# Two decoder layers on one core: the S5 rotation goes back into PSUM with three drive banks, the S5 set-up is reordered, and the conditioning bias is spread over four column groups

## The reference

```python
mod = c_act @ w_ada[layer] + b_ada[layer]          # c_act = silu(c), 6*1024 columns a layer
sh_m, sc_m, gt_m, sh_f, sc_f, gt_f = split(mod, 6)
u = rms_norm(h, g_mix) * (1 + sc_m) + sh_m
```

```python
# S5, a group g of 16 channels with 64 states; dt = exp(log_dt)
mag = exp(lr * dt);  abar = mag * (cos(li*dt), sin(li*dt))
den = lr*lr + li*li;  nr = abar_r - 1
fr = (nr*lr + abar_i*li) / den;  fi = (abar_i*lr - nr*li) / den
bbar_r = fr*br - fi*bi;  bbar_i = fr*bi + fi*br
bu = ug @ bbar                                     # "drive"
x[t] = abar * x[t-1] + bu[t]                       # complex
y = xr @ c_re - xi @ c_im + d * ug                 # "read-out" and "skip"
y = gelu(y);  y = y * sigmoid(y @ w_glu + b_glu)
```

## Time and profile before

| | |
|---|---|
| median of three runs | 1721.92 us (1721.36 to 1724.17) |
| profiled execution | 1726.36 us |
| its span, first to last instruction | 1724.5 us |
| TensorE busy | 1609.7 us, 93% |
| VectorE busy | 1270.1 us, 74% |
| ScalarE busy | 1044.6 us, 61% |
| GpSimd busy | 79.2 us, 5% |
| mean granted clock of TensorE | 0.962 |

### The profile page before, as it was taken

How to read it: one execution, slowest core, us unless ns; L and a number is a source line. 1 busy time by engine, 2 the same in 40 slices (tenths; PEclk the granted TensorE clock), 3 DMA queues, 4 the chain that set the end, 5 groups by cost and what they waited for, 6 DMA issues and landing times.

```text
span 1724.5 us, 22990 instructions
## 1 busy us (share of the span) xinstructions
PE 1609.7 (93%) x7839; PEld 1269.1 (74%) x7840; DVE 1270.1 (74%) x1753; ACT 1044.6 (61%) x1401; POOL 79.2 (5%) x101
## 2 busy tenths in 40 slices
PE   4989979999898896899999999999999999999996
PEld 2535559999695554788888888888888888888885
DVE  6786245555445313889989989989989989989986
ACT  2203334444342542778878778778778778778775
POOL 7442000000000000000000000000000000000000
PEclk9889989999898897899999999999999999999998
DMA  9523745555653555699999999999999989999960
GB/s 324 205 98 123 286 165 177 183 177 184 227 189 106 189 194 205 227 359 340 349 347 356 353 349 348 352 332 372 354 332 363 357 334 365 353 336 369 347 246 26
DMA packets 208054, 469.66 MB, mean 272 GB/s; under 512 B 5316, under 2 KB 26102, under 8 KB 207878
## 3 DMA queue, kind: packets, MB, share of 16 engines
q1 hardware_dynamic: 206960, 466.80, 74.9%
q0 software_dynamic: 400, 1.09, 0.3%
q10 hardware_dynamic: 646, 1.16, 0.2%
HBM read 467.98 MB, written 1.05 MB: 272 GB/s over the span
## 4 chain that ended last, share of the span: by engine, by line
PE 84%; DVE 7%; ACT 3%; issue 2%; DMA 1%; SPq 1%; DVEq 0%; POOL 0%; ACTq 0%
PE ps L790 22%; PE ps L792 21%; PE ps L791 21%; PE ps L796 3%; PE ps L813 2%; PE ps L1283 2%; DVE w_lo L1798 2%; PE ps L857 2%; PE ps L1054 2%; ACT work L1694 1%; DMA ring<-in_w_ada 1%; PE ps L974 1%; PE ps L945 1%; PE ps L871 1%; PE ps L925 1%
## 5 line engine op out<-in xcount | busy, mean ns | idle before, releaser
L1798 DVE TENSOR_TENSOR w_lo<-ring,w_hi 128x1024 fp32r<-128x1024 f32 (+4 forms) x600 | 672.8, 1154 | 92.0 <-ACT w_hi L1488 79.1
L1488 ACT ACTIVATE w_hi<-ring 128x1024 fp32r<-128x1024 f32 (+4 forms) x600 | 601.2, 1008 | 216.8 <-PE ps L792 214.5
L790 PE MATMUL ps<-w_hi,e_hi 128*128 128x512 f32 x896 | 356.7, 398 | 9.7 <-DVE w_lo L1798 9.7
L792 PE MATMUL ps<-w_hi,e_lo 128*128 128x512 f32 x896 | 350.7, 391 | 0.0
L791 PE MATMUL ps<-w_lo,e_hi 128*128 128x512 f32 x896 | 349.8, 390 | 0.0
L1798 DVE TENSOR_TENSOR w_lo<-ring_more,w_hi 128x1024 fp32r<-128x1024 f32 x192 | 228.9, 1221 | 40.5 <-ACT w_hi L1488 38.1
L1488 ACT ACTIVATE w_hi<-ring_more 128x1024 fp32r<-128x1024 f32 x192 | 201.6, 1067 | 70.7 <-PE ps L792 70.7
L790 PEld LDWEIGHTS ps<-w_hi,e_hi 128*128 128x128 f32 x896 | 168.9, 188 | 46.1 <-DVE w_lo L1798 13.2
L792 PEld LDWEIGHTS ps<-w_hi,e_lo 128*128 128x128 f32 x896 | 168.6, 188 | 36.6
L791 PEld LDWEIGHTS ps<-w_lo,e_hi 128*128 128x128 f32 x896 | 169.1, 189 | 33.6
L790 PE MATMUL ps<-w_hi,eT_hi 128*128 128x512 f32 x448 | 176.7, 395 | 5.6 <-DVE w_lo L1798 5.6
(11 more groups left out here) (281 smaller groups left out, 1743.5 us busy)
## 6 DMA issues: line engine op xcount, KB each, us to landing
ring<-in_moe_w_gate SPq DMA_DIRECT2D x48, 2048.0 KB, 9.8
ring<-in_moe_w_up SPq DMA_DIRECT2D x40, 2048.0 KB, 10.1
ring<-in_moe_w_down SPq DMA_DIRECT2D x32, 2048.0 KB, 10.0
ring<-in_w_ada SPq DMA_DIRECT2D x24, 2048.0 KB, 8.7
ring_more<-in_moe_w_down SPq DMA_DIRECT2D x24, 2048.0 KB, 7.8
ring_more<-in_moe_w_up SPq DMA_DIRECT2D x16, 2048.0 KB, 9.9
ring_more<-in_moe_w_gate SPq DMA_DIRECT2D x8, 2048.0 KB, 9.4
ring<-in_ff_w_gate SPq DMA_DIRECT2D x8, 1408.0 KB, 6.3
```

Of the source, the lines that this page charges most:

```text
L790: mm(o, xh, wh, start=start, stop=False)
L792: return mm(o, xl, wh, start=False, stop=stop)
L1488: fn(w, src, ACT.Copy).then_inc(hi_ready, 1)
L1798: V.tensor_tensor(w_lo[0:n, c, 0:f], src, w_hi[0:n, c, 0:f].bitcast(F32), ALU.subtract).then_inc(lo_ready, 1)
```

## The change

**Turn.** The sine product goes to `rotB` in SBUF as before; then the cosine product is written over the drive in its own PSUM bank, and the sum and the difference read that bank and `rotB`. The bank is free behind the difference. There are three drive banks (6, 4, 5) instead of two.

**Order on TensorE.** The S5 transposes go ahead of the S5 projection, the first two drives ahead of its last quarter, and `qkv` starts behind it; queries and keys are transposed at the end, into banks 2 and 3. On VectorE the skip and the rotary pieces are one to two turns later.

**Set-up.** GpSimd's eleven small operations for `fr` and `fi` go to VectorE, between its levels 2 and 3; `bbar` follows on GpSimd ahead of its last two powers. ScalarE makes the pads between its second and third part copy. The bias rows are loaded first.

**Bias.** The four bias matmuls of a product go to the four column groups instead of all to the first.

```diff
@@ sync
-            load(static_before[0])
             sp.dma_start(bias_rows[0:BROWS, :], A["b_ada"].rearrange("l (k p) -> (l k) p", p=P)).then_inc(bias_in, 16)
-            for e in static_before[1:n_first]:
+            for e in static_before[:n_first]:
@@ gpsimd
-            for n in range(NLEV - 1):
+            def power(n):
...
-            pool.wait_ge(s5_mag, 1)
-            mul(par(AR), par(MAG), powers[:, 0, 0, :])
-            mul(par(AI), par(MAG), powers[:, 0, 1, :])
-            affine(par(NR), par(AR), 1.0, -1.0)
-            pool.wait_ge(s5_rden, 1)
-            for o, a, b, c, d, last_op in ((FR, NR, LR, AI, LI, add), (FI, AI, LR, NR, LI, sub)):
-                mul(par(TT), par(a), par(b))
-                mul(par(T2), par(c), par(d))
-                last_op(par(o), par(TT), par(T2))
-                mul(par(o), par(o), par(RDEN))
+            for n in range(5):
+                power(n)
             pool.wait_ge(s5_in, 16 * 4)
+            pool.wait_ge(f_ready, 1)
...
+            for n in range(5, NLEV - 1):
+                power(n)
@@ tensor
                 for q in range(4):
-                    w = mm(ps[bank][0:32, q * P:(q + 1) * P], ident[0:BROWS, row + q:row + q + 1].broadcast_to([BROWS, 32]),
-                           bias_rows[0:BROWS, :], start=False, stop=q == 3, tile_position=(0, 0))
+                    j = 32 * q
+                    w = mm(ps[bank][j:j + 32, q * P:(q + 1) * P], ident[0:BROWS, row + q:row + q + 1].broadcast_to([BROWS, 32]),
+                           bias_rows[0:BROWS, :], start=False, stop=True, tile_position=(0, j))
...
-                if j >= 2:
-                    pe.wait_ge(bu_used, j - 1)
+                if j >= 3:
+                    pe.wait_ge(bu_used, j - 2)
...
-                    w = mm(ps[(6, 4)[j % 2]][:, i * S:(i + 1) * S], s5_bT[r, i, j // 4, :], s_inT[r, j // 4, :], start=True,
+                    w = mm(ps[(6, 4, 5)[j % 3]][:, i * S:(i + 1) * S], s5_bT[r, i, j // 4, :], s_inT[r, j // 4, :], start=True,
...
-            qkv(0)
-            qkv(1)
+            s_proj(0)
+            s_proj(1)
+            s_proj(2)
             drive(0)
             drive(1)
+            s_proj(3)
+            drive(2)
             for jp in range(8):
-                for s in range(6 * jp + 2, min(6 * jp + 8, 48)):
+                for s in range(6 * jp, 6 * jp + 6):
                     qkv(s)
-                if jp < 7:
-                    drive(2 * jp + 2)
-                    drive(2 * jp + 3)
+                for j in (2 * jp + 3, 2 * jp + 4):
+                    if j < NCH:
+                        drive(j)
                 if jp:
                     read_out(2 * jp - 2)
-                if jp == 6:
-                    qk_transposes(0, (5, 2))
-                    qk_transposes(1, (3, 5))
+            qk_transposes(0)
+            qk_transposes(1)
@@ scalar
-            for i in range(4):
+            for i in range(2):
+                part_out(i, parts0[:, i, :], 4 + i)
+            pads()
+            for i in range(2, 4):
                 part_out(i, parts0[:, i, :], 4 + i)
             norm_out(0)
-            pads()
+            s5_weights()
@@ vector
-            for n in range(5):
+            for n in range(3):
+                level(n)
+            dve.wait_ge(s5_mag, 1)
+            step(V.tensor_tensor(par(AR), par(MAG), powers[:, 0, 0, :], ALU.mult))
+            chained(V.tensor_tensor(par(AI), par(MAG), powers[:, 0, 1, :], ALU.mult))
+            chained(V.tensor_scalar(par(NR), par(AR), -1.0, None, ALU.add))
+            dve.wait_ge(s5_rden, 1)
+            for o, a, b, c, d, last_op in ((FR, NR, LR, AI, LI, ALU.add), (FI, AI, LR, NR, LI, ALU.subtract)):
+                step(V.tensor_tensor(par(ER), par(a), par(b), ALU.mult))
+                chained(V.tensor_tensor(par(EI), par(c), par(d), ALU.mult))
+                chained(V.tensor_tensor(par(o), par(ER), par(EI), last_op))
+                w = V.tensor_tensor(par(o), par(o), par(RDEN), ALU.mult)
+                if o == FR:
+                    chained(w)
+                else:
+                    w.then_inc(f_ready, 1)
+            for n in range(3, 5):
                 level(n)
...
-                step(V.tensor_tensor(rotA, bu, c(0), ALU.mult))
-                V.tensor_tensor(rotB, bu, c(1), ALU.mult).then_inc(bu_used, 1)
+                chained(V.tensor_tensor(rotB, bu, c(1), ALU.mult))
+                chained(V.tensor_tensor(bu, bu, c(0), ALU.mult))
+                step(V.tensor_tensor(s5_v[:, 0, :], bu[:, 0, :], rotB[:, 1, :], ALU.add))
+                V.tensor_tensor(s5_v[:, 1, :], bu[:, 1, :], rotB[:, 0, :], ALU.subtract).then_inc(bu_used, 1)
+                step.wait()
                 dve.wait_ge(bu_used, j + 1)
-                step(V.tensor_tensor(s5_v[:, 0, :], rotA[:, 0, :], rotB[:, 1, :], ALU.add))
-                chained(V.tensor_tensor(s5_v[:, 1, :], rotA[:, 1, :], rotB[:, 0, :], ALU.subtract))
...
-                if j % 4 == 1 and j >= 5:
+                if j % 4 == 2 and j >= 6:
                     y_before_gelu(j // 4 - 1)
-                if j in (5, 6, 10, 11):
+                if j in (7, 8, 12, 13):
```

More of the change, by code:

```diff
@@ L290, in trunk @@
         powers_ready = sem("powers_ready")
+        f_ready = sem("f_ready")
         late_in = sem("late_in")
@@ L801, in s5_transposes @@
                 for i, bank in enumerate((5, 6, 7, 4)):
+                    if i == 3:
+                        pe.wait_ge(mod_ready, 1)
                     pad = (b_pad, c_pad)[i // 2]
@@ L813, in matvec @@
                     w = mm(ps[bank][j:j + 32, :], c_col[:, k:k + 1].broadcast_to([P, 32]), ap[:, k, :],
-                           start=k < 4, stop=k > 4, tile_position=(0, j))
+                           start=k < 4, stop=False, tile_position=(0, j))
                     if k == 0:
@@ L918, in _, with s_proj @@
             columns_of(3, parts0[:, 3, :], 4, 12).then_inc(mod_summed, 1)
+            pe.wait_ge(part_ready, 4)
+            s5_transposes()
             pe.wait_ge(uT_ready, 8)
-            ap, got = e_in[3]
-            arrived(got)
-            for c in range(4):
+            def s_proj(c):
+                ap, got = e_in[3]
+                if c == 0:
+                    arrived(got)
                 for k in range(KD):
```

32 lines of the change are left out of this document (15 added, 17 removed).

## The result

The changed kernel takes 1699.01 us (median of 4 runs, 1697.09 to 1702.33) beside 1723.05 us for the kernel before (median of 4, 1721.36 to 1725.53): ratio 0.9863, 95% interval 0.9846 to 0.988. Run again later, beside three of the experiments, it took 1701.22 us (1699.95 to 1702.05), ratio 0.9872, 0.9852 to 0.9891. So it is faster by 21 to 24 us. The forecast was 1701, range 1693 to 1712.

A forecast was written before the change was run, and what follows sets the result against it. The prediction took a chain alternating between TensorE and VectorE, then TensorE's, as the bound. Terms 3.1 - 7.6 - 8.4 - 8.2 = -21.1 took the profiled 1726.36 to 1705.3, or 1701 against the median 1721.92; range 1693 to 1712.

The forecast's parts named there:

- Set-up, +3.1: Start to modulation columns: VectorE's added small operations and its waits beside GpSimd cost 3.1 us, bounds +0.7 and +3.7.
- Ahead of the loop, -7.6: Input ready to first S5 turn: transposes moved into idle time, 16 passes fewer beforehand; 13.7 us instead of 21.26.
- Rival 3: Set-up and S5 projection: GpSimd costs VectorE nothing, TensorE's clock stays at 2.4 GHz; 1696 us, chance 0.08.
- Turns, -8.4: The 16 S5 loop turns: 256-element operations stop waiting for GpSimd; 71.7 us against 80.1.
- the 2.0 forecast at turn 6: S5 loop: first skip operation wants the second read-out at about 87.7, TensorE has it at 89.7; 2.0 us wait.
- Bias, -8.2: Attention conditioning products: bias matmuls over four column groups save 0.55 us each, on 15 products of the chain.
- my fullest case: Bias of one conditioning product: eight rows take 0.27 us if four run at a time, 0.43 if two.
- The nine others: Conditioning products outside the 15 counted on the chain, taken to lie beside loads or VectorE and save nothing.
- Rival 1: Conditioning products: short bias rows stay at 0.107 us each, so the bias gains nothing; 1709 us, chance 0.16.
- rival 2: S5 loop: TensorE becomes the bound, its clock falls in gaps of six rounds, adding 10 us; 1711, chance 0.12.
- Rival 4: S5 turns: writing the product into the PSUM bank it is read from is slow, +22 us; 1723, chance 0.04.
- sum of -21.1: Whole kernel: set-up, stretch ahead of the loop, turns and bias together, taken from the profiled execution of 1726.36 us.

The follow-up runs named there:

- the first trace: Trace of the changed kernel's first measurement, unaltered, from its fastest run, 1697.09 us; span 1695.3.
- the second trace: Trace of the changed kernel run again, unaltered, beside later experiments: 1701.22 us, ratio 0.9872 to the kernel before; span 1699.5.

## Why the prediction was right

**Set-up, +3.1:** +2.5 and +3.4. The waits beside GpSimd's six operations came as taken: six operations of VectorE lose 0.3 to 0.5 each (0.94 for a free 0.44 at 23.91), 2.4 in all, and moving the six away moves the waits along. In the traces with the columns behind the level's second operation they are at 44.84 to 46.17, around the forecast 45.8.

**Ahead of the loop, -7.6:** -8.0 with the low clock at the projection's start, which the forecast assumed, and -9.5 without it. Rival 3 had this half right: the full clock does come, in some executions. The transposes' place is worth 4.7 to 5.1.

**Turns, -8.4:** -7.9 and -7.6. The pieces: the 256-element operation at 0.42 beside GpSimd, as said; the free turn 3.62 for 3.53 (+1.4 over 16); the scans +0.1 for +0.18 (-0.6); 0.95 + 0.96 of waits at turns 5 and 6 for the 2.0 forecast at turn 6. The cause of the first of the two was not foreseen: a late product of GpSimd beside a scan. Of the gain, writing back is 4.8 (77.24 with both products in SBUF, 72.46 without), and the third bank and the new places of the skip and rotary pieces are the first 2.9 (80.10 to 77.24); the new places were not tried alone. (The turn at 74.20, which the prediction calls the fourth, is the third; its reading holds.) That an input in PSUM costs VectorE nothing more was a choice, and the rows bear it out: 0.42 with one input in PSUM, and 0.42 with none in the earlier trace rows. By the estimate from the figures of the Trainium skill weighed there ("VectorE: DVE Perf Modes", § The TRN2 errata) the former would be 0.065 us longer; the rows do not agree.

**Bias, -8.2: the step that was mis-sized.** Two errors, both to the same side. Eight rows take 0.22, not 0.30 (0.63 saved in place of 0.55), that is 0.028 a row: four at a time and nothing else, below my fullest case of 0.27. And 17 products are on the chain, not 15. "The nine others lie beside loads or VectorE" was wrong for the two at the end of the dense SwiGLU, which the chain of the changed kernel still has:

```profile
415.31 0.22 PE ps L814 x8
415.53 1.72 PE ps L808 x16
417.24 0.26 PE ps L814 x8
```

17 x 0.63 = 10.7, 2.5 more than forecast. The stretch that holds the products shortened by 12.5 in the mean of the traces; the other 1.8 is where no bias row is. Rival 1 fell with the first row. The rule that stood for it (the Trainium skill, "TensorE: Matmul & The Clock Gate", Part 3: a weight load overlaps matmuls in flight only when the row group differs) is not what these rows show, and that the bias would gain nothing by it was the prediction's inference. All of a product's bias matmuls use the same row groups, and in four column groups they take a quarter of the time, with their loads. Four of the loads in the first trace run from 146.57 to 146.70 us, while the matmuls of the product ahead (145.25 to 147.17), which use these row groups too, are in flight.

**TensorE as the bound (rival 2):** half true, in another form. It is busy from 47.5 to 101 us without a gap and its clock mostly stays up in the loop (the one read-out of 3.17 in the second trace stands behind a gap of 0.68), so the 10 us of that rival did not come. But taking VectorE's two waits out by other rounds, with and without earlier first drives, did not bring the gate forward. After the last scan VectorE waits 2.9 to 3.2 us for TensorE's scores in the changed kernel, 8.28 in the two with other rounds, and nothing in before. The change brought the stage close to the point where both engines are the limit.

**Rival 4** is out by its row: 0.70 for a product written to the PSUM bank that it is read from.

So the sum of -21.1 against the traced execution is -25.0 in the changed kernel's second trace: bias -4.1, ahead of the loop -0.4, behind the last scan -1.0 (the last read-out at 1.92 instead of 3.33), turns +0.8, set-up +0.3, the end +0.6. Against the medians the forecast 1701 lies between 1699.01 and 1701.22. That it is so near is in part luck. The terms fall short of the traces by 3.9, most of it the bias; beside the medians only 1 to 3 us of this is left, since the traced run of before is 3.3 to 4.4 above its median. What is not settled: why the stretch between the SwiGLU and the second attention varies by 5 us, and whether the two halves of the change overlap.

## What to carry to other kernels

Count the repeats of a small item on the chain before sizing the item: the bias matmuls, 0.85 us each time, gave half of the whole gain, and the error in them was as much the number of times as the duration. When one of two engines in a loop is made faster, ask for the other's sum of work over the stage, not only for the waits: a wait that goes in one turn comes back at the stage's end if the other engine has no slack. And work that was on the path is worth placing in a gap of TensorE (4.7 to 5.1 us here); work added only to keep the clock up was not (2.0 us lost for 1.7 won).

## What the runs showed of the hardware

- The same instructions of the same kernel began at either level of TensorE's clock from one execution to the next: 48 passes took 10.63 us behind a gap of 0.78, and 12.21 behind gaps of 0.59 and 0.85. A forecast of such a stretch needs both.
- GpSimd and VectorE hold each other up when VectorE's inputs are both in SBUF, and it goes both ways: with VectorE's 512-element operations at 1.10 in the set-up, GpSimd's 256-element addition took 1.06, where it took 0.78 beside 256-element operations in the changed kernel.
- Four float32 matmuls of 128 columns (eight rows of the trace) took 0.22 us together in four column groups, and 0.85 in one.
- VectorE writes 512 elements into the PSUM bank that it reads them from in 0.70 us, as fast as into SBUF (0.69).
